# A one-hot product for the first expert's rows, and a new order of the router's conditioning tiles, in a two-layer decoder step

## What is computed

```
def moe_swiglu(h, w_router, b_router, w_gate_up, w_down):
    logits = (h @ w_router).astype(jnp.float32) + b_router.astype(jnp.float32)
    top_val, top_idx = lax.top_k(logits, TOP_K)
    top_w = jax.nn.softmax(top_val, axis=-1)
    ...
    for e in range(N_EXPERTS):
        y = y + gates[..., e:e + 1] * swiglu(h, w_gate_up[e], w_down[e])

x = x + g2[:, None, :] * f
shf, scf = jnp.split(jax.nn.silu(c) @ p['final_ada_w'] + p['final_ada_b'], 2, axis=-1)
y = modulate(rmsnorm(x, p['final_norm']), shf, scf)
```

## Time and profile before

| | us |
|---|---|
| median of 3 runs | 1775.8 (1775.76 to 1776.41) |
| the profiled execution, own time | 1775.7 |
| its span, first to last instruction | 1774.0 |
| TensorE busy | 1618.1 (91%) |
| DVE busy | 1263.9 (71%) |
| ACT busy | 1079.6 (61%) |

### The profile page before, as it was taken

One profiled execution on the slowest core, in us unless ns is written; L12 is line 12 of the kernel. 1 busy time (PEld: TensorE's weight loads), 2 busy tenths in 40 slices (PEclk: granted clock), 3 DMA queues, 4 the chain that ended last, 5 costly groups with the idle time before them and its releaser, 6 DMA issues.

```text
span 1774.0 us, 25158 instructions
## 1 busy us (share of the span) xinstructions
PE 1618.1 (91%) x9156; PEld 1308.3 (74%) x9156; DVE 1263.9 (71%) x1433; ACT 1079.6 (61%) x1309; POOL 88.9 (5%) x135
## 2 busy tenths in 40 slices
PE   5799786999986799599999999999999999999992
PEld 2695265999976667278888888888888888888882
DVE  2463354554565724389899899899998998998982
ACT  2553133443452453477777777777777777777771
POOL 2000101000002400100000000000000000000001
PEclk9899887999998899899999999999999999999995
DMA  9266977555557887699999999999999999999972
GB/s 347 76 211 231 387 262 257 188 174 177 178 190 289 321 323 255 251 352 361 369 378 375 376 369 377 380 371 366 382 372 372 373 376 380 367 366 387 373 279 97
DMA packets 241091, 546.24 MB, mean 308 GB/s; under 512 B 6131, under 2 KB 28785, under 8 KB 241026
## 3 DMA queue, kind: packets, MB, share of 16 engines
q1 hardware_dynamic: 229202, 504.42, 78.4%
q0 software_dynamic: 11184, 38.75, 5.9%
q10 hardware_dynamic: 640, 2.18, 0.4%
HBM read 522.56 MB, written 22.75 MB: 307 GB/s over the span
## 4 chain that ended last, share of the span: by engine, by line
PE 83%; DMA 7%; DVE 5%; ACT 3%; issue 2%; POOL 1%; SPq 0%; another core or an unknown queue 0%; ACTq 0%; DVEq 0%; POOLq 0%
PE psum L733 24%; PE psum L734 24%; PE psum L735 24%; DMA ring<-in_ada_w 3%; PE psum L704 2%; DMA ring<-in_cache_k 2%; PE psum L1168 1%; DMA ring<-in_ffn_w_gate_up 1%; PE psum L723 1%; DVE w_lo L1604 1%; DVE ring L1883 1%; DMA ring<-in_gla_w_in 1%; PE psum L688 1%; PE psum L972 1%; ACT w_hi L1247 0%
## 5 line engine op out<-in xcount | busy, mean ns | idle before, releaser
L2055 DVE TENSOR_TENSOR w_lo<-ring,w_hi 128x1024 fp32r<-128x1024 f32 x672 | 814.2, 1224 | 81.7 <-ACT w_hi L1546 64.7
L1546 ACT CAST w_hi<-ring 128x1024 fp32r<-128x1024 f32 x672 | 706.6, 1054 | 206.2 <-PE psum L735 200.1
L733 PE MATMUL psum<-w_hi,xe_hi 128*128 128x512 f32 x896 | 359.9, 402 | 3.2 <-DVE w_lo L2055 3.2
L735 PE MATMUL psum<-w_hi,xe_lo 128*128 128x512 f32 x896 | 355.8, 397 | 0.0
L734 PE MATMUL psum<-w_lo,xe_hi 128*128 128x512 f32 x896 | 355.7, 397 | 0.0
L733 PE MATMUL psum<-hh,w_hi 128*128 128x264 f32 x864 | 252.8, 293 | 32.4 <-DVE w_lo L1604 19.7
L1604 DVE TENSOR_TENSOR w_lo<-ring,w_hi 128x1024 fp32r<-128x1024 f32 (+1 forms) x132 | 160.2, 1222 | 151.6 <-ACT w_hi L1247 151.4
L734 PE MATMUL psum<-hl,w_hi 128*128 128x264 f32 x864 | 249.2, 288 | 0.0
L735 PE MATMUL psum<-hh,w_lo 128*128 128x264 f32 x864 | 249.1, 288 | 0.0
L1247 ACT CAST w_hi<-ring 128x1024 fp32r<-128x1024 f32 (+1 forms) x132 | 135.6, 1034 | 127.7 <-PE psum L735 86.0
L733 PEld LDWEIGHTS psum<-w_hi,xe_hi 128*128 128x128 f32 x896 | 169.3, 189 | 42.5 <-DVE w_lo L2055 3.5
(11 more groups left out here) (347 smaller groups left out, 1421.3 us busy)
## 6 DMA issues: line engine op xcount, KB each, us to landing
ring<-in_moe_w_gate_up SPq DMA_DIRECT2D x112, 2048.0 KB, 9.2
ring<-in_moe_w_down SPq DMA_DIRECT2D x56, 2048.0 KB, 8.4
ring<-in_ada_w SPq DMA_DIRECT2D x24, 2048.0 KB, 10.9
ring<-in_ffn_w_gate_up SPq DMA_DIRECT2D x22, 1024.0 KB, 8.9
ring<-in_gla_w_in SPq DMA_DIRECT2D x6, 2048.0 KB, 11.2
ring<-in_kv_ada_w SPq DMA_DIRECT2D x4, 2048.0 KB, 8.0
ring<-in_ffn_w_down SPq DMA_DIRECT2D x4, 2048.0 KB, 7.9
ring<-in_kv_w SPq DMA_DIRECT2D x4, 2048.0 KB, 12.8
```

Source lines behind the costliest of these rows:

```text
L733: eng.matmul(to, wh, ah, start=start, stop=False)
L735: return eng.matmul(to, wl, ah, start=False, stop=stop)
L1546: eng.copy(unit(w_hi, kind, n), quarter(ring[(BASE + j // 4) % RING], kind, j % 4)).then_inc(S["hi_ready"], 1)
L2055: eng.tensor_tensor(unit(w_lo, kind, n), quarter(ring[(BASE + j // 4) % RING], kind, j % 4), unit(w_hi, kind, n), ALU.subtract).then_inc(S ...
```

## The change

Tiles 28 and 29 are both run ahead of the router product and turned behind it, tile 30 runs ahead of the counts, tile 31 and the turns of 30 and 31 behind them; tiles 30 and 31 get banks 0 and 1. Four of the six turns of h move behind the counts. ACT loads the table for silu ahead of the branch rather than behind it. DVE makes `pick`, for each token a row of 128 with a 1 at its slot if expert 0 has it. In `Else` TensorE multiplies `h_tok` by `pick`, 24 products, which gives expert 0's rows already turned, in place of reading them from `routed`; the scratch rows serve experts 1 to 7. The 16 transposes of x and their four copies move behind the experts' loop. The gain rows go through bank 3 in place of 4.

```diff
-ADA_GROUPS = (..., (28, (2, 3)))
+ADA_GROUPS = (..., (28, (2, 3)), (30, (0, 1)))
# POOL
-                expert_rows(0)
+                expert_rows(1)
...
-                eng.wait_ge(S["xe_turned"], 2)
-                expert_rows(1)
# TensorE
-            ada(112, 116)
+            eng.wait_ge(S["ada_kept"], 28)
+            ada_whole(28)
+            ada_whole(29)
...
-            turn_h(0)
-            turn_h(1)
+            ada_turn(28)
+            ada_turn(29)
             eng.wait_ge(S["lg_kept"], 1)
...
-            for i in range(2, 2 * TT):
-                turn_h(i)
+            turn_h(0)
+            turn_h(1)
+            ada_whole(30)
...
-            ada(116, 128, ends=True)
+            for i in range(2, 2 * TT):
+                turn_h(i)
+            ada_whole(31)
+            ada_turn(30)
+            ada_turn(31)
...
-                eng.wait_ge(S["ada_kept"], 32)
-                for i in range(4):
-                    t, a = i // 2, i % 2
-                    for j in range(4):
-                        last = eng.transpose(pb[i][:, j * P:(j + 1) * P], x[:, 4 * a + j, t * P:(t + 1) * P], ident[:])
-                    last.then_inc(S["once_turned"], 1)
+                eng.wait_ge(S["rows_placed"], 2)
+                eng.wait_ge(S["h_tok_kept"], 2 * TT)
+                for a in range(2):
+                    for k in range(4):
+                        for t in range(TT):
+                            n, c = TOK[t], 4 * a + k
+                            last = eng.matmul(pb[7 - 3 * a][:, k * CAP:(k + 1) * CAP], h_tok[0:n, t, c * P:(c + 1) * P],
+                                              pick[0:n, t, :], start=t == 0, stop=t == TT - 1)
+                    last.then_inc(S["xe_turned"], 1)
...
-                eng.wait_ge(S["expert_rows"], 16)
-                eng.wait_ge(S["once_kept"], 5)
-                turn_rows(0)
...
+                                if p == 1:
+                                    eng.wait_ge(S["once_kept"], 1)
...
-                            eng.wait_ge(S["expert_rows"], it * 16 + 32)
-                            turn_rows(it * 2 + 2)
+                            eng.wait_ge(S["expert_rows"], it * 16 + 16)
+                            turn_rows()
# behind the loop: the 16 transposes of x, as above
# ACT
-            norm(FFN1, splits=False, after=(S["kept_dve"], empt[-1][1]), during=(112, 116))
+            norm(FFN1, splits=False, after=(S["kept_dve"], empt[-1][1]), during=(112, 120))
+            ada_copy(29)
...
-            ada(116, 128, ends=True)
+            ada_copy(30)
+            eng.preload_act_table_set("silu_and_others")
+            for i in range(2, 2 * TT):
+                keep_h_tok(i)
+            ada_copy(31)
...
-                eng.preload_act_table_set("silu_and_others")
                 keep_gathered(0)
+                eng.wait_ge(S["once_turned"], 1)
+                eng.copy(last_kept, pb[3][0:KC, 0:3 * P]).then_inc(S["once_kept"], 1)
...
# DVE
+            ada_add(28)
+            ada_add(29)
...
+            for t in range(TT):
+                n = TOK[t]
+                last = eng.scalar_tensor_tensor(pick[0:n, t, :], iota[0:n, 0:CAP], slot_f[0:n, t, 0:1],
+                                                chosen[0:n, t, 0:1].to_broadcast([n, CAP]), ALU.is_equal, ALU.mult)
+            last.then_inc(S["rows_placed"], 1)
...
-            ada(116, 128, ends=True)
+            ada_add(30)
+            ada_add(31)
...
+                    eng.wait_ge(S["once_kept"], 5)
```

More of the change, by code:

```diff
@@ L277, in build @@
         h_tok = st_sb(stage, "h_tok", [P, TT, D])
+        pick = st_sb(stage, "pick", [P, TT, CAP])
         gathered = ExitStack()
@@ L689, in ada_turn, with ada_strips @@
                 last.then_inc(S["ada_turned"], 1)
+            def ada_strips(i, half):
+                for g in range(STRIPS):
+                    k = half * STRIPS + g
+                    last = eng.matmul(pb[ADA_BANKS[i]][g * STRIP:(g + 1) * STRIP, :], c_pad[:, k, :],
+                                      cols8(slot("ada", i))[:, k, :], start=half == 0, stop=half == 1)
+                    if half == 1:
+                        last.then_inc(S["ada_done"], 1)
             def ada(lo, hi, ends=False):
@@ L701, in ada @@
                     if j % 2 == 1:
[L702 to L707, removed]
+                        ada_strips(i, j // 2)
                     if j == 1 and i not in ADA_STARTS:
@@ L1154, in _, with turn_rows @@
                                          mod[:, SHIFT[FINAL]:SHIFT[FINAL] + KC, 0])):
-                    last = eng.transpose(pb[4][0:KC, n * P:(n + 1) * P], row, ident[:])
+                    last = eng.transpose(pb[3][0:KC, n * P:(n + 1) * P], row, ident[:])
                 last.then_inc(S["once_turned"], 1)
-                def turn_rows(done):
+                def turn_rows():
                     for a in range(2):
@@ L1208, in _ @@
                             eng.wait_ge(S["at_lo_ready"], it * 7 + 7)
-                            eng.wait_ge(S["expert_rows"], it * 16 + 32)
-                            turn_rows(it * 2 + 2)
+                            eng.wait_ge(S["expert_rows"], it * 16 + 16)
+                            turn_rows()
+                for i in range(4):
+                    t, a = i // 2, i % 2
+                    for j in range(4):
+                        last = eng.transpose(pb[i][:, j * P:(j + 1) * P], x[:, 4 * a + j, t * P:(t + 1) * P], ident[:])
+                    last.then_inc(S["once_turned"], 1)
                 eng.wait_ge(S["last_gains"], 1)
@@ L1495, in _, with keep_h_tok @@
             eng.preload_act_table_set("natural_log_exp_and_others")
-            for i in range(2 * TT):
+            def keep_h_tok(i):
                 t, a = i // 2, i % 2
@@ L1521, in _ @@
             with eng.Else():
[L1522 to L1527, removed]
-                eng.dma_start(last_rows.rearrange("n (k p) -> k n p", p=P),
-                              last_kept.rearrange("k (n p) -> k n p", n=3)).then_inc(S["last_sent"], 16)
                 def keep_gathered(done):
@@ L1565, in _ @@
                 eng.copy(y_e[:], psum[:, 5 * 512:7 * 512]).then_inc(S["y_e_kept"], 1)
+                for i in range(4):
+                    eng.wait_ge(S["once_turned"], i + 2)
+                    eng.copy(x_tok[:, i // 2, i % 2 * 512:(i % 2 + 1) * 512], pb[i]).then_inc(S["once_kept"], 1)
                 def root_of(t):
```

12 lines of the change are left out of this document (11 added, 1 removed).

## The result

The kernel got slower: 1780.45 us (median of 17 runs, 1776.82 to 1784.82) against 1775.88 us (17 runs, 1774.38 to 1777.23). The ratio is 1.0025, with an interval of 1.0017 to 1.0032. The forecast was 1773.0, its range ended at 1776.8, and slower had a chance of 0.04. The profiled execution took 1776.8 us (span 1775.0), the shortest of the 17.

The account below looks back on a forecast made before the run. Bound: the bridge between last norm and first expert matmul, and the tail. Root +1.9, order and code -6.7, branch 0, work behind it +2.1 gave -2.7 us: 1775.7 to 1773.0, range 1769.5 to 1776.8.

Parts of the forecast that it names:

- Bound, expert loop, tail: Time can move only in the bridge and the tail; expert loops have no gap, turning x in the tail costs nothing.
- Part 1: Tile 29 ahead of the router product: ACT's root waits for a copy, so root and router product come 1.9 us later.
- Part 2: TensorE's order up to the branch: last turn and load of the count at 732.1 instead of 736.89, 4.8 us earlier.
- rival B: TensorE waits for code again ahead of the branch: +2.1 us, 1775.1; chance 0.17.
- Part 3: Load of the count and branch to the first matmul behind: 8.2 us as before, ends 4.5 and 8.2.
- Rival A: The branch gets cheap with fewer transfers in flight, half of 6.16 us goes: -3.1 us, 1769.9; chance 0.23.
- Part 4: Behind the branch: 48 product records take 7.4 us, ends 5.2 and 11.0; first expert matmul at 752.3 against 755.0.
- rival C: The clock stays low through the products: 11.0 us instead of 7.4, 1776.6; chance 0.10.
- Part 5: Expert 0 and tail: same low-clock stretch, 1 us either way; x turned in the tail under DVE's DMA wait, costing nothing.
- Rival D: Slower: TensorE waits 6.2 us for code within the products, rest at low clock 3.6: +9.8 us, 1782.8; chance 0.04.
- The serial part on ACT behind the products: Cast, gain-row copy, DMA issue and loop entry put the first weight split at 749.9; first matmul 2.37 us after it.
- Taking the row transfer away alone is worth about nothing.: In the bridge, PE waits only 1.42 us for expert rows, and ACT is in its table load until 751.66 anyway.

Follow-up runs that it names:

- the padded kernel: Changed kernel with the third token tile zero-filled and all products run over 128 rows: 1772.32 us, ratio 0.9979 to the kernel before.
- the two quiet kernels: The padded kernel with scatter and third weight tile held until behind the branch, without and with the root first: 1771.01 us (0.9975) and 1768.98 us (0.9963).

## Why the prediction was wrong, by its steps

**Bound, expert loop, tail.** Right. The time was decided in the bridge alone. In the tail DVE still waits for the gathered rows when x has long been turned and copied, which answers the earlier trace rows:

```profile
1734.60 1.91 PE L1233 MATMUL psum<-ident,x 128*128 128x128 f32 x16
...
1735.71 2.06 ACT L1596 COPY x_tok<-psum 128x512 f32<-128x512 f32 x4
...
1747.55 1.28 DVE L2121 SCALAR_TENSOR_TENSOR x_tok<-ring,w,x_tok 128x1024 f32<-128x1024 f32 x1 [10.47 <-DMA ring<-expert_gated,row_back]
```

The copies took 2.06 us for four; they end at 1737.8, ten before DVE needs them.

**Part 1, the root 1.9 later.** Right. ACT after:

```profile
709.29 0.59 ACT L1286 COPY ada_row<-psum 128x512 f32<-128x512 f32 x1 [4.30 <-PE psum L694]
709.77 0.43 ACT L1317 ACTIVATE rstd<-rstd 128x264 f32<-128x264 f32 x1
```

The root starts 6.20 us after the squares, before 4.36 (709.61 - 705.25): 1.84. Taking the copy out of its way gave that back.

**Part 2, the order.** Right, and the code wait at tile 31 did not come back (rival B falls): from the end of the router product to the last turn 728.95 - 717.89 = 11.1 us, where I had 11.0. The 1.4 us beyond my -4.8 are the router product at the high clock in this profile, which is luck; in the kernel with the order alone, with the router product at the low clock (5.41 us), the load of the count comes 26.81 us after the squares, where I had 26.85, and in the padded kernel (5.11) 26.53. One reading was wrong without effect: before the change the scatter does not start at 725 but at 727.74, released by `row_of`, and after it at 727.22. In the kernel with the product alone, with the old order, tile 31's last turn comes at 736.25, 1.85 us after its strips began, and 736.89 - 733.09 = 3.8 before. So part of that wait goes even with the old order, and what sets it is not settled.

**Part 3, the branch 8.2.** It was 9.2, and I had chosen the upper end. Rival A, that the branch gets cheaper with less in flight, fell: the third weight tile and the scatter held TensorE up for 6.95 us, where it had been 6.16 with three tiles and the end of the scatter. My reason was right (both are in flight); the size was off by 0.8, which lies within what the row varies between kernels with both in flight (6.66 to 7.62). My lower end of 4.5 for a branch with no bulk transfer ahead of the code had no row behind it; the two quiet kernels give 4.47 and 4.62 for load and branch together. The rule of the Trainium skill ("DMA: Bandwidth & Descriptors", Queues, rings and completion order), that an engine takes turns between its rows by the packet, so that it matters whether another row has work and not how much, agrees for the weight tiles: 6.16 with three tiles and the end of the scatter, 6.37 with one alone, 3.43 and 3.58 with none. It does not tell why the scatter costs a fifth of what the weight tile does at the same load of the engines (4.09); that stays open. That a taken branch to a target outside the pages at hand costs a fetch by DMA (the Trainium skill, "Runtime: NRT & Kernel Launch", Instruction fetch mechanics) agrees as well: with all else quiet the 3.4 to 3.6 us stay, and one packet of q8 and one of q14 move in them. Of these 3.4 to 3.6 us, 1.0 lies ahead of the packet of q8, 0.9 to 1.0 is the packet, and 1.55 comes behind it.

**Part 4, the products 7.4, ends 5.2 and 11.0. This is the step that failed**: 15.03, past both ends. The count was right (48 records), and so was the time of one record at either clock: with 128 rows throughout, the block took 7.39 us in one kernel, 7.4 as forecast, and 7.1 to 8.2 over the six kernels that have them, by the moment at which the clock rose (3.1 to 5.5 us after its start). Two terms were missed:
- the changes of the row count. At the low clock the block takes 10.57 us without a change (all 8 rows) and 15.03 with them (8 or 64 rows in turns): 4.5 us. The single records of the trace show where it is: starts lie 0.213 us apart between records of like shape, and 0.35 to 0.375 at the records at and behind a change. Each group of six then takes 1.87 us in place of 1.28.
- the clock. 10.57 - 7.39 = 3.2 us in the block is the low clock staying (2.6 against the padded kernel's 8.02). That is rival C (I had 11.0 for the block, and a chance of 0.10), and it came true on top of the other. Behind the block it cost nothing more: the clock is low for the first 2.9 us of expert 0 (757.6 to 760.5), before the change it was for 4.3 (755.0 to 759.3), and expert 0 is 0.6 us shorter. Part 5, which expected the same stretch within 1 us, holds.

My sum took the record time from a block of one shape and held it for a block that alternates between two. No row on which the sum rests has such an alternation, and the upper end of 11.0 took in the clock alone. A term whose pattern the trace does not show was to be bounded further off. Rival D had the right place and sign and another mechanism, a wait for code inside the block; there is none, TensorE is busy through it.

**The serial part on ACT behind the products** was forecast as 2.1 to the first weight split and 2.37 more, 4.4 to 4.5 from the end of the products; measured 757.64 - 753.20 = 4.4. Right.

**"Taking the row transfer away alone is worth about nothing."** Right for the old order only in the part that was argued: the rows' path had 1.4 us of wait. With the new order it has 4.45, and the order needs the product to be worth anything. I had added the two gains as if each stood alone; here they didn't, but the sum that I made was of both together, so this did no harm.

**The sum by what was measured:** root +1.8, order and code -6.7 (and -1.4 of clock), branch +1.0, behind it +9.6: +4.3. With the products at 7.4 it would have been -3.3, an estimate, of which 1.4 is the luck of the clock; the padded kernel, with 8.0, took 3.1 us less than the kernel before on its chip by the medians and 3.7 by the ratio.

What stays open: in the changed kernel itself, whether the clock stays low because of the pauses at the changes or because of the third of its products that has few rows. Dense 8-row products keep it low without any pause, 64-row ones with pauses keep it low as well. The kernel with the 8-row products together has the same third of 8-row products and three changes in place of fifteen, and its clock rose 8.5 us after the block's start, where the changed kernel's rose only after 22 (738.2 to 760.5, 4 us of them idle). So the changes have a part in it, and the few rows, by the padded kernel's 5.0, may have one too; but grouping also puts the 128-row products in long runs, and no kernel parts the three. Open too is what sets the clock in the router product (3.96 to 5.42 us between profiles), and why the changed kernel's runs lie over 8 us (1776.8 to 1784.8) where those of before lie over 2.9 on the same chip. In the three later comparisons the runs of before lie over 6 to 8 us, and those of the changed kernel, in one of them, over 4.5, so this need not be the change. And what TensorE does in the 0.3 us at a change no run here shows.

## What to carry to other kernels

Short matmuls that differ in their number of rows should be padded to one row count, or at least grouped: it costs a memset and it saved 7 of 15 us here (grouping 5). When a gain is to come from letting one engine get somewhere earlier, ask what the next one to arrive is and take both steps together: here the order was worth 0 without the product and 4 with it. Around a taken branch, keep weight loads out of flight and start them right behind it, but not together with everything else that was held back. A single profile holds the luck of the clock: compare the parts of it that an edit can touch, and leave the total to the medians.

## What the runs showed of the hardware

- A change of the active row count between two f32 matmuls (128 to 8, or 128 to 64, and back) puts the next records 0.35 to 0.375 us after the one before, at the low clock, in place of 0.213, 0.3 us for each change; the size of the change makes no difference (15.03 us for the block in both). At the high clock one change, in the kernel with the 8-row products together, gave 0.205 and 0.213 in place of 0.112.
- 10.57 us of back-to-back products over 8 rows ran at a granted clock of 0.50 (1.2 GHz) to their end; in products over 128 rows the clock rose to the full 2.4 GHz 3.1 to 5.5 us after their start (six kernels; in one of them it had been high for the first four records).
- This taken branch costs TensorE 3.4 to 3.6 us with the DMA engines idle, 4.1 beside an indirect scatter, and 6.2 to 7.6 beside a weight tile. The differences lie ahead of the packet of the instruction queue; 1.4 to 1.6 us pass from its end to the end of the row in all the kernels named.
- DVE waits as long at the same branch, but not in its branch row: that takes 72 ns, and the next operation starts 6.4 us later in the changed kernel (731.5 to 737.9) and 3.0 us later with both transfers late (732.6 to 735.6).
- The register load ahead of the branch takes TensorE 0.49 us without the scatter in flight (three kernels, in one of them beside a weight tile), 1.03 beside the scatter alone, and 1.17 to 1.70 beside scatter and tiles.
